# Norm scaling and paired squares laid out over a group's eight output blocks, in a two-layer hybrid trunk on eight cores

## The reference

```python
def rms_norm(x, g):
    y = xf * lax.rsqrt(jnp.mean(xf * xf, axis=-1, keepdims=True) + EPS)
    return (y * g).astype(x.dtype)

for l in range(DEPTH):                       # 2
    sh_m, sc_m, g_m, sh_f, sc_f, g_f = jnp.split(silu(c) @ w_ada[l] + b_ada[l], 6)
    h = modulate(rms_norm(x, norm_mix_g[l]), sh_m, sc_m)      # h * (1 + scale) + shift
    x = x + g_m * hybrid_mixer(h, ...)       # three attentions, gated sum, @ w_out
    h = modulate(rms_norm(x, norm_ffn_g[l]), sh_f, sc_f)
    x = x + g_f * swiglu(h, w_ffn_in[l], w_ffn_out[l])        # hidden 2816
return rms_norm(x, final_norm_g)
```

## Time and profile before

| | us |
|---|---|
| median of three runs | 3057.37 (2710.59 to 3122.42) |
| the profiled execution | 2688.61 |
| its span on the slowest core | 2687.1 (eight cores: 2675.7 to 2687.1) |
| TensorE busy | 2543.1 (95%) |
| VectorE, ScalarE, POOL busy | 1084.4, 1034.2, 278.9 |

### The profile page before, as it was taken

The page is one execution under the profiler, slowest core; times in us unless marked ns, Lnnn a source line. Parts: engine busy times, 40 slices in busy tenths (PEclk is TensorE's granted clock), DMA queues, the critical chain, the costliest instruction groups (busy, mean ns, idle before and its releaser), DMA issues.

```text
span 2687.1 us, 41392 instructions; the slowest of 8 cores (2675.7 to 2687.1 us)
## 1 busy us (share of the span) xinstructions
PE 2543.1 (95%) x15104; PEld 1233.7 (46%) x15104; DVE 1084.4 (40%) x1615; ACT 1034.2 (38%) x1390; POOL 278.9 (10%) x342
## 2 busy tenths in 40 slices
PE   3889999989999999999989999999999999999998
PEld 1435555544444444444443455555444444444443
DVE  2553443444445423232264444354444462222316
ACT  2466776662223410101144677766422243011012
POOL 2411000000001200000130100000000030000002
PEclk8899999999999999999999999999999999999999
DMA  9203321202225343433431001022122243222213
GB/s 214 47 15 61 65 37 25 64 13 36 36 39 139 57 85 56 71 63 63 87 111 29 16 14 21 17 62 31 18 36 36 47 121 55 40 40 40 40 32 126
DMA packets 66517, 148.02 MB, mean 55 GB/s; under 512 B 6592, under 2 KB 19456, under 8 KB 64272
## 3 DMA queue, kind: packets, MB, share of 16 engines
q0 software_dynamic: 55712, 99.76, 23.3%
q1 hardware_dynamic: 10608, 45.61, 4.8%
HBM read 228.12 MB, written 16.97 MB: 91 GB/s over the span
## 4 chain that ended last, share of the span: by engine, by line
PE 88%; issue 3%; DMA 3%; DVE 3%; ACT 3%; DVEq 0%; POOL 0%; ACTq 0%; POOLq 0%
PE ps L380 71%; PE ps L378 16%; DMA sb_WS<-wada 1%; DMA sb_WS<-win 1%; DVE sb_OS L409 1%; ACT sb_PT L390 1%; ACT sb_RD L390 1%; DVE sb_XT L399 0%; ACT sb_HT L390 0%; DVE sb_W L403 0%; DVE sb_TMPF L399 0%; DVE sb_RD L394 0%; DMA sb_WS<-wfi 0%; DVE sb_W L409 0%; ACT sb_TMPF L390 0%
## 5 line engine op out<-in xcount | busy, mean ns | idle before, releaser
L380 PE MATMUL ps<-sb_HT,sb_WS 128*128 128x512 bf16 (+1 forms) x5760 | 1331.3, 382 | 33.9 <-DMA sb_WS<-win 11.8
L380 PEld LDWEIGHTS ps<-sb_HT,sb_WS 128*128 128x128 bf16 (+1 forms) x5760 | 549.8, 98 | 701.5 <-issue 75.4
L390 ACT ACTIVATE sb_TMPF<-ps 128x512 f32<-128x512 f32 x388 | 231.2, 597 | 1136.1 <-PE ps L380 1134.3
L390 ACT ACTIVATE sb_PT<-ps 128x1024 bf16<-128x1024 f32 (+1 forms) x494 | 483.9, 986 | 311.6 <-PE ps L378 308.6
L380 PE MATMUL ps<-sb_W,sb_WS 128*128 128x512 bf16 x1920 | 418.0, 379 | 0.8 <-DVE sb_W L394 0.7
L378 PE MATMUL ps<-sb_PT,sb_W 128*128 128x512 bf16 (+4 forms) x1212 | 283.4, 339 | 46.4 <-DVE sb_OS L409 21.2
L394 DVE TENSOR_TENSOR sb_W<-ps,sb_TMPF 128x512 bf16<-128x512 f32 x176 | 121.4, 692 | 483.7 <-PE ps L380 471.5
L380 PEld LDWEIGHTS ps<-sb_W,sb_WS 128*128 128x128 bf16 x1920 | 187.5, 98 | 226.8 <-issue 1.8
L378 PE MATMUL ps<-sb_W 128*128 128x512 bf16 (+7 forms) x1212 | 257.4, 339 | 0.0
L399 DVE SCALAR_TENSOR_TENSOR sb_XT<-ps,sb_modT,sb_XT 128x512 f32<-128x512 f32 x256 | 186.5, 748 | 154.3 <-PE ps L380 154.0
L409 DVE CAST sb_W<-ps 128x512 bf16<-128x512 f32 (+1 forms) x176 | 121.2, 690 | 261.7 <-PE ps L380 252.2
(11 more groups left out here) (57 smaller groups left out, 1221.2 us busy)
## 6 DMA issues: line engine op xcount, KB each, us to landing
sb_WS<-wada POOLq DMA_DIRECT2D x48, 512.0 KB, 8.4
sb_WS<-wfi POOLq DMA_DIRECT2D x44, 512.0 KB, 5.3
sb_WS<-wmg POOLq DMA_DIRECT2D x48, 384.0 KB, 5.0
sb_XT<-x SPq DMA_DIRECT2D x8, 2048.0 KB, 18.7
sb_WS<-win POOLq DMA_DIRECT2D x60, 256.0 KB, 4.5
sb_WS<-wfo POOLq DMA_DIRECT2D x24, 512.0 KB, 5.3
xs<-sb_XT SPq DMA_DIRECT2D x4, 2048.0 KB, 6.8
sb_XT<-xs SPq DMA_DIRECT2D x4, 2048.0 KB, 16.3
```

The source lines that it names most:

```text
L380: r = e.matmul(o, lhsT=l, rhs=rr, start=st, stop=sp)
L390: return P.op("act", lambda e, o=out, i=in_, f=func, kw=kw: e.activation(out=o, in_=i, func=f, **kw), reads=reads, writes=writes)
```

## The change

Inside `out_group` the norm of group g-1 is now spread: RS after block 1, then two scalings after each of the evictions 2 to 5. The squares of group g are recorded block by block by the new `square`. In mode "pair", after each odd block: ScalarE squares the even chunk into OS (fp32), POOL squares the odd chunk into RD (fp32), and POOL adds both into one bf16 tile of PT; so RS is 4 matmuls with ones in place of 8. The last FFN group of layer 0 has mode "act" (eight ScalarE squares, eight matmuls), the last of layer 1 "one" (as before: even ones on ScalarE, odd ones on POOL, eight matmuls). The norms of the prologue are as they were.

```diff
     def norm_rs(g, used):
-            pe_group([(PS[bi][:, :], onesb[:, :], PT[:, i, :], c == 0, c == NCH - 1)], [ptb[i], onesbuf], [psb[bi]])
+            pe_group([(PS[bi][:, :], onesb[:, :], PT[:, i, :], c == 0, c == len(used) - 1)], [ptb[i], onesbuf], [psb[bi]])
...
-    def norm_scale(g, gs_ap, sh_ap, vec_bufs, dst=None, pool=False):
+    def norm_scale(g, gs_ap, sh_ap, vec_bufs, dst=None, pool=False, cs=range(NCH)):
         ri = g % 2
-        for c in range(NCH):
+        for c in cs:
...
-    def out_group(wos, nk, src, srcb, g, gcol, mid=None):
+    def square(g, c, mode):
+        if mode == "pair":
+            if c % 2 == 0:
+                return []
+            i = next_rot("pt", 8)
+            q = (c // 2) % 2
+            act(OS[:, q, :], XT[g][:, c - 1, :], AF.Square, [xt[c - 1][g]], [osb[q]])
+            tt(RD[:, q, :], XT[g][:, c, :], XT[g][:, c, :], ALU.mult, [xt[c][g]], [rdb[q]], eng="pool")
+            tt(PT[:, i, :], OS[:, q, :], RD[:, q, :], ALU.add, [osb[q], rdb[q]], [ptb[i]], eng="pool")
+            return [i]
+        i = next_rot("pt", 8)
+        if mode == "act" or c % 2 == 0:
+            act(PT[:, i, :], XT[g][:, c, :], AF.Square, [xt[c][g]], [ptb[i]])
+        else:
+            tt(PT[:, i, :], XT[g][:, c, :], XT[g][:, c, :], ALU.mult, [xt[c][g]], [ptb[i]], eng="pool")
+        return [i]
+
+    def out_group(wos, nk, src, srcb, g, gcol, prev, vecs, dst=None, mode="pair"):
+        used = []
...
-            if dco == 1 and mid is not None:
-                mid()
+            if prev is not None and dco == 1:
+                norm_rs(*prev)
+            if prev is not None and 2 <= dco <= 5:
+                norm_scale(prev[0], *vecs, dst=dst, cs=(2 * dco - 4, 2 * dco - 3))
+            used += square(g, dco, mode)
+        return (g, used)
...
-            out_group(wos, 8, MG, mg, g, (l, 16),
-                      None if prev is None else lambda prev=prev: norm_fin(prev[0], prev[1], *ffnv(l)))
-            prev = (g, norm_sq(g))
+            prev = out_group(wos, 8, MG, mg, g, (l, 16), prev, ffnv(l))
...
+                    prev = out_group(wos, nj, ATv, atb, g, (l, 40), prev, mixv(l + 1), None, "pair" if g + 1 < NG else "act")
                     P.dma("sp", lambda e, g=g: e.dma_start(out=xs_d[g], in_=XTf[g]), xsd[g], reads=xtg(g))
-                    prev = (g, norm_sq(g))
...
+                    prev = out_group(wos, nj, ATv, atb, g, (l, 40), prev, (gfin, None, [cb]), fin_dst, "pair" if g + 1 < NG else "one")
```

More of the change, by code:

```diff
@@ L1063, in tail @@
                 for g in range(NG):
-                    out_group(wos, nj, ATv, atb, g, (l, 40),
-                              None if prev is None else lambda prev=prev: norm_fin(prev[0], prev[1], *mixv(l + 1)))
+                    prev = out_group(wos, nj, ATv, atb, g, (l, 40), prev, mixv(l + 1), None, "pair" if g + 1 < NG else "act")
                     P.dma("sp", lambda e, g=g: e.dma_start(out=xs_d[g], in_=XTf[g]), xsd[g], reads=xtg(g))
-                    prev = (g, norm_sq(g))
                 state["last"] = prev
@@ L1086, in tail @@
                 for g in range(NG):
-                    out_group(wos, nj, ATv, atb, g, (l, 40),
-                              None if prev is None else lambda prev=prev: norm_fin(prev[0], prev[1], gfin, None, [cb], fin_dst))
-                    prev = (g, norm_sq(g))
+                    prev = out_group(wos, nj, ATv, atb, g, (l, 40), prev, (gfin, None, [cb]), fin_dst, "pair" if g + 1 < NG else "one")
                 norm_fin(prev[0], prev[1], gfin, None, [cb], fin_dst)
```

## The result

The changed kernel takes 2733.17 us (median of 5 runs), the kernel before 2712.49 on the same chip: ratio **1.0063, 95% interval [1.0033, 1.0092]**, slower. The ratio is not the quotient of these two medians (1.0076), since it leaves out executions in which one die ran much slower at a lower granted clock (one of 3066 us on the second occasion had a die at 0.85; for the 3057 us ahead of the prediction no clock is on record).

A forecast was written before the change was run, and what follows sets the result against it. TensorE's matmuls bound the kernel; stage losses 13.0 + 6.8 + 8.1, plus 7.3 for POOL's forms, less 8.5 for the win wait, gave +26.7 us on 2688.61: 2715 us. Range 2678 to 2744, the forecast itself 2701 to 2722.

The forecast's parts named there:

- TensorE sets the pace before and is made to wait after: Output groups: TensorE's matmuls set the pace before; after the change it waits 3 to 5 us per loop at ones matmuls.
- The loop: From one norm's last ones matmul to the next one's, through VectorE, ScalarE and POOL: 17.9 us, of which collisions 3.2.
- POOL's new forms: Paired multiply and add on POOL: 1.15 us each, the middle of 1.04 and 1.26, adding 7.3 us.
- The stages: Losses with POOL at 1.04: output projections 6.5 us each, FFN of layer 0 6.8, of layer 1 8.1.
- The win gain: End of layer 0's FFN: win loads no longer queue behind POOL's squares, 7.83 + 1.3 - 0.6 = 8.5 us gained.
- The clock: Clock lowered by stalls: nothing counted in the loops; a few microseconds at a stage's end belong to the upper side.
- No case but B leaves that band: slower 0.05, faster 0.01, same 0.94: Chances of the measured verdict, taking 2% (54 us) as about what a measurement tells from no change.
- B: Rival: evictions also collide once POOL writes fp32, six more collisions per loop, 38 us, 2753 us; chance 0.05.
- C: Rival: the win wait stays because transfers, not POOL's queue, are late; +8.5 us, 2724 us; chance 0.08.
- D: Rival: scalings and POOL instructions exclude each other for their whole times, 0.33 us more per collision, 2726 us; chance 0.05.
- A: Rival: collisions are rare because POOL and VectorE fall into step; loop 14.7 us, 2674 us in all; chance 0.13.
- matmul end to RS in use: 1.73: First term of the loop: from a norm's last ones matmul until the scalings can use RS, 1.73 us.

The follow-up runs named there:

- change_again: The changed kernel once more, nothing edited, against the kernel before on the same chip: 2714.24 against 2688.37 us, ratio 1.0097.
- act_last: The kernel before with only the squares of the last group of layer 0's FFN moved from POOL to ScalarE: 2678.76 us, ratio 0.9959.
- rs_psum: The changed kernel with RS of the spread scalings written to the PSUM bank of its own sum: 2679.83 us, ratio 0.9963 to the kernel before.

## Why the prediction was right in its steps and wrong in its chances

- **TensorE sets the pace before and is made to wait after**: held. Waits for POOL's sums 2.0 us before, 31.9 after.
- **The loop**: forecast 17.9 with POOL at 1.04, near 18.65 with 1.15; measured on core 0 18.84 and 19.07 in the projections, 19.05 and 19.74 in the FFN of layer 0, 17.80 and 17.53 in that of layer 1. The forecast's terms against the first loop of core 0 (854.02 to 872.86):

| term | forecast | measured |
|---|---|---|
| ones matmuls' end to the first scaling | 1.73 | 2.80 |
| VectorE until its last scaling ends (867.13), collisions with it | 10.9 | 10.3 |
| ScalarE's last HT and square of block 4, until POOL's add (868.67) | 1.5 | 1.5 |
| POOL's add, multiply, add (to 872.33) | 3.4 (1.04 each) | 3.7 |
| to the end of the last ones matmul | 0.4 | 0.5 |

  The term that was too small is the first. 1.73 was read off the second norm of the earlier trace rows; the first norm there, like every stage's first, has the table load in it (857.54 to 860.34, 2.80). The collisions, forecast 3.2, lost 2.96 in this group. The second loop has no table load, but its eviction of block 2 comes 1.0 us behind RS, 0.6 of it by the clock. So two unforeseen terms of about 1 us, one in each loop, stand behind 18.8 and 19.1 in place of 17.9, and that 18.65 lies close to them is in part luck.
- **POOL's new forms**: the multiply takes 1.04 and the add 1.26 alone. The 1.15 taken was wrong for both and right for their mean, by luck. What decides is whether the two inputs are one tile or two, as in the earlier trace rows; the fp32 output of the multiply costs nothing. The floor that the prediction took from the Trainium skill (2.5 cycles an element, 1.07 us; on that page it stands under Instruction dispatch, while the section named measures 2.6) gives both forms one price, and the rows have 1.04 and 1.26.
- **The stages**, change_again core 2 against before core 0, with the 7.3 for POOL shared out: projection of layer 0, forecast +8.4, measured +8.1; of layer 1, +8.4 and +6.1; FFN of layer 1, +10.0 and +10.4; FFN of layer 0 with the win gain, -0.2 and +0.2. Sum 26.7 and 24.8. The 2.7 us of lag at a projection's end came in layer 0 (norm 2 to the last group's norm 21.45 us for 19.30) and not in layer 1 (18.48 for 18.99).
- **The win gain**: forecast 8.5, measured 10.3 by act_last on core 0; of the 0.6 us of waiting kept in the sum nothing came, and the 24 matmuls behind the old wait had lost more to the clock there (8.19 us, where the earlier trace rows have 6.62).
- **The clock**: "I count nothing" was nearly right in the loops (19.07 for 18.84) and wrong at the stage's end on some cores. Core 0 waits 3.17 us for the last evictions, and the next 32 matmuls take 9.96 us where 32 x 0.216 + 0.16 is 7.07:

```profile
905.45 9.96 PE L380 MATMUL ps<-sb_HT,sb_WS 128*128 128x512 bf16 x32 [3.17 <-DVE sb_XT L399]
```

In change_again cores 1 and 6 show the same 10 us behind the same wait, and the other six 7.07; this is the few microseconds of the upper side, and which core pays them is chance.
- **The lower end, 2701**: its own terms don't give it. With POOL at 1.04 (7.3 less) and half of 8 loops' collisions missing (8 x 1.6 = 12.8 less) the sum is 2695.
- **The base**: 2715 was 2688.61 + 26.7. On the first occasion both kernels lay higher (2712.49 and 2733.17), and the sum is made for the difference, not for that level.

**The step that failed** is "No case but B leaves that band: slower 0.05, faster 0.01, same 0.94", and its ground, "2% (54 us) is about what a measurement tells from no change". No run supports that ground. Comparable executions of the kernel before on one chip span 2684.95 to 2690.22 us, 0.2%, and the ratios above come with intervals of 0.1 to 0.3% to either side. The three times shown ahead (2710.59 to 3122.42) are no measure of it. Against such a measurement the forecast's own 1.0% is a clear loss, as are C and D; of all the cases only A stood on the other side. The same five cases would have given about 0.87 for slower. The mechanism and its place were there, the size was near (+25.9 and +20.7 by the medians of the two comparisons, for +26.7), and the conclusion drawn from them was of the wrong resolution. Inside the sum the step that was mis-sized is "matmul end to RS in use: 1.73", 2.80 in the first loop of each stage.

Of the signs, "scalings averaging over 1 us" held only for the spread ones: the mean of all 120 is 0.981 (core 0), and with the 48 others at 0.917, as in rs_psum, the 72 spread ones come to an estimated 1.02. Of the rivals, A was wrong at its premise (the scalings did collide), B's evictions stayed at 0.747 us on average (0.748 before), C fell with act_last. D's price per collision was too high: a pair of scalings lost 1.04, 0.78, 0 and 1.14 us, together less than the 3.2 taken.

## What to carry to other kernels

Before spreading one engine's work among another's, draw the loop that this closes, from one product back to the next one of its kind, and add up every engine in it: 12 us of matmuls saved were nothing against loops 3 to 5 us longer than TensorE's own work. Where VectorE and POOL meet in such a loop, look whether one of VectorE's SBUF operands can live in PSUM (36 us here), keep the last link of the loop the shortest form of the work (a single square in place of a pair, with the squares issued sooner: 24 us), add the loads of ScalarE's tables to the links (1.28 us in each stage's first loop), and see that no load stands in a queue behind arithmetic that it doesn't need (10 us). When an experiment moves work ahead, count the tiles of its rings again: a square written a block too early made three of the kernels above wait, and add the wrong square. And take the size of "no change" from how closely comparable executions agree, not from the spread of a few times of mixed kind.

## What the runs showed of the hardware

- A two-input POOL instruction on 128x512 fp32 takes 1.04 us when both inputs are one tile and 1.26 when they are two, whatever the output (1.04 with fp32 and with bf16).
- A VectorE instruction with two SBUF tiles and a POOL instruction take turns (scaling pairs 2.18 to 2.54 us for 1.40); with one tile in PSUM both keep their durations (0.743; 1.039 and 1.270), over 72 scalings and 112 POOL instructions.
- ScalarE's table load ahead of the first Ln of an output stage took 1.28 us, and RS came 2.69 us after the ones matmuls and not 1.47, in the kernels before and after.
- Behind waits of 3 to 4 us TensorE's next matmuls ran in part at 1.2 GHz on some cores: behind 4.22 us the granted clock was 0.77 over 7.3 us and 1.7 us were lost, behind 3.17 us at the stage's end it was 0.70 over 10 us and 2.9 us were lost. Behind the same wait of 3.16 us on core 2 of change_again nothing was lost (32 matmuls in 7.07 us).
- The granted clock also fell with no wait ahead: core 5 of the first comparison, busy without a gap from 815 us on, took 20.81 us for the first 80 matmuls of the output projection (842.85 on, granted clock 0.83), for which cores 1, 2 and 3 took 17.43.
